# A sixth buffer for the experts' down weights, the overflow table summed on TensorE, and another order of capacities in a one-core decoder step

## The reference

```python
def moe(h, w_router, b_router, we_g, we_u, we_d, ws_g, ws_u, ws_d):
    s = jax.nn.sigmoid(jnp.dot(h, w_router).astype(jnp.float32))
    ...                                   # group-limited top-8 of 64 experts for each token
    def step(acc, blk):
        e, tok, wt = blk                  # expert, its rows of h, their weights
        xb = h[tok]
        hb = jax.nn.silu(xb @ we_g[e]) * (xb @ we_u[e])
        return acc.at[tok].add(wt[:, None] * (hb @ we_d[e]).astype(jnp.float32)), None
    ...
    shared = (jax.nn.silu(h @ ws_g) * (h @ ws_u)) @ ws_d
    return (routed + shared.astype(jnp.float32)).astype(h.dtype)
```

## Time and profile before

| | |
|---|---|
| profiled execution | 1106.16 us |
| its span (first to last instruction of the profile) | 1104.3 us |
| median of three runs | 1107.29 us |
| PE busy | 1063.3 us (96%) |
| VectorE busy | 730.3 us (66%) |
| first gate/up matmul of block 0 | 487.64 us |
| last down matmul of block 47 ends | 1041.1 us |
| moved by DMA in the whole execution | 337.11 MB |

### The profile page before, as it was taken

How to read it: one execution, slowest core, us unless ns; L and a number is a source line. 1 busy time by engine, 2 the same in 40 slices (tenths; PEclk the granted TensorE clock), 3 DMA queues, 4 the chain that set the end, 5 groups by cost and what they waited for, 6 DMA issues and landing times.

```text
span 1104.3 us, 16558 instructions
## 1 busy us (share of the span) xinstructions
PE 1063.3 (96%) x5950; PEld 533.5 (48%) x5950; DVE 730.3 (66%) x1935; ACT 215.4 (20%) x473; POOL 135.6 (12%) x163
## 2 busy tenths in 40 slices
PE   6999999999999999999999999999899999999896
PEld 3456678777877644664433333333233333333232
DVE  3218441546545645766988888888687988888167
ACT  4131332222232313301111111111010111111111
POOL 0110000000020010111111111111111212121100
PEclk9999999999999999999999999999999999999999
DMA  9858720120352267769999999999999999999698
GB/s 368 340 200 302 241 81 27 50 86 1 115 191 87 77 243 249 284 281 382 413 411 425 421 426 425 424 422 425 425 425 425 421 424 424 413 417 407 261 417 353
DMA packets 51653, 337.11 MB, mean 305 GB/s; under 512 B 9636, under 2 KB 14088, under 8 KB 30830
## 3 DMA queue, kind: packets, MB, share of 16 engines
q1 hardware_dynamic: 33710, 287.32, 64.1%
q0 software_dynamic: 17856, 48.68, 11.5%
HBM read 311.30 MB, written 37.24 MB: 316 GB/s over the span
## 4 chain that ended last, share of the span: by engine, by line
PE 82%; DMA 11%; DVE 4%; issue 1%; ACT 1%; SPq 0%; DVEq 0%; ACTq 0%
PE bank L1599 24%; PE bank L1622 13%; PE bank L1294 10%; DMA mem<-in_w_exp_down 6%; PE bank L1313 5%; PE bank L1412 3%; DMA hT<-in_w_exp_down 3%; PE bank L1413 3%; PE bank L1207 3%; PE bank L1530 3%; PE bank L1291 3%; DMA mem<-expert_out_rows 2%; PE bank L1708 2%; PE bank L1182 1%; PE bank L1610 1%
## 5 line engine op out<-in xcount | busy, mean ns | idle before, releaser
L1599 PE MATMUL bank<-mem 128*32 128x512 f32 (+2 forms) x1568 | 334.0, 595 | 1.8 <-DVE mem L2291 1.0
L2291 DVE STREAM_TRANSPOSE mem<-mem 32x256 f32<-32x256 f32 x448 | 195.1, 436 | 5.8
L1622 PE MATMUL bank<-mem 128*32 128x512 f32 (+2 forms) x712 | 178.7, 602 | 9.2 <-DMA mem<-in_w_exp_down 5.7
L1599 PEld LDWEIGHTS bank<-mem 128*32 128x32 f32 (+2 forms) x1568 | 106.9, 128 | 165.0 <-issue 164.9
L1294 PE MATMUL bank<-hT,mem 128*128 128x288 f32 x512 | 133.3, 410 | 1.0 <-ACT mem L973 1.0
L2291 DVE STREAM_TRANSPOSE mem<-x_sb 32x256 f32<-32x256 f32 x240 | 104.5, 435 | 3.1
L1294 PEld LDWEIGHTS bank<-hT,mem 128*128 128x128 f32 x512 | 93.8, 190 | 25.8 <-issue 2.4
L1622 PEld LDWEIGHTS bank<-mem 128*32 128x32 f32 (+2 forms) x712 | 56.6, 132 | 80.3 <-issue 71.2
L1599 PE MATMUL bank<-x_sb,mem 128*32 128x512 f32 (+2 forms) x256 | 87.1, 596 | 0.0
L2307 DVE COPY hT<-bank 128x512 f32<-128x512 f32 x48 | 33.2, 691 | 66.6 <-PE bank L1622 66.5
L827 POOL DMA_INDIRECT mem<-ffn_in_rows,idxg x32 | 33.0, 1030 | 268.2 <-DVE idxs L2275 192.8
(11 more groups left out here) (398 smaller groups left out, 1215.5 us busy)
## 6 DMA issues: line engine op xcount, KB each, us to landing
mem<-k_w_exp SPq DMA_DIRECT2D x54, 2048.0 KB
mem<-in_w_exp_down SPq DMA_DIRECT2D x52, 1024.0 KB
x_sb<-k_w_exp SPq DMA_DIRECT2D x10, 2048.0 KB
mem<-k_w_ada SPq DMA_DIRECT2D x8, 2048.0 KB, 9.3
mem<-k_w_in SPq DMA_DIRECT2D x7, 2048.0 KB, 9.5
hT<-in_w_exp_down SPq DMA_DIRECT2D x12, 1024.0 KB
mem<-expert_out_rows SPq DMA_DIRECT2D x6, 2048.0 KB, 18.1
mem<-k_w_head SPq DMA_DIRECT2D x4, 2048.0 KB, 17.2
```

Of the source, the lines that this page charges most:

```text
L1599: i = mm(bank[sl, :], xT[:, j % 2, c * BLK + sl.start:c * BLK + sl.stop], gu_view(r)[:, c, :], start=c == 0, stop=c == KC - 1)
L1622: i = mm(ps[4 + hf][sl, :], hhT[:, k * BLK + sl.start:k * BLK + sl.stop], dn_view(r)[:, k, hf * 512:(hf + 1) * 512], start=k == 0, stop=k ...
L2291: i = dve.transpose(cols[dl, :, sl], rows[sl, :, dl])
```

## The change

Four things are changed.

1. `CAPS` has other numbers in another order, and `PRE` is `[0, 1, 5, 21]` in place of `[0, 1, 4, 5]`. The sum is 192 units as before, and the multiset of the 60 capacities outside `PRE` is the same (7, 6, four 5s, nine 4s and so on). The blocks that the two tables give are: before 18 whole, 12 in two pieces of 64, 18 in four of 32; after 8 whole, 11 in two, 29 in four. The fourth preloaded expert is first used in block 15.
2. The down weights get a sixth place: 2048 columns of `aux`, which held the router's scratch. The scratch that is left moves behind column 3072.
3. The large operations of `table` go. VectorE makes two columns on 64 partitions, TensorE sums over the partitions with two small matmuls behind the down matmuls of block 4, and VectorE finishes the table in block 6.
4. SyncE reads a rank's expert number (a TENSOR_LOAD) ahead of each load in place of once a rank, and issues the down loads of free places ahead of the wait for the shared expert.

```diff
-PRE = [0, 1, 4, 5]
-CAPS = [4, 4, 2, 2, 4, 4, 2, 2, 2, 2, 4, 5, 3, 4, 3, 5, 2, 2, 3, 1,
+PRE = [0, 1, 5, 21]
+CAPS = [4, 4, 1, 2, 4, 4, 1, 3, 2, 2, 4, 4, 3, 3, 3, 3, 4, 2, 2, 3,
...
-WSLOTS = 5
+WSLOTS = 6
...
-        DN_AT = [gate_at, 2 * KC * FE, WSZ + 2 * KC * FE, w2_at, None]
+        DN_AT = [gate_at, 2 * KC * FE, WSZ + 2 * KC * FE, w2_at]
...
-        assert at <= NO * NE
-        ocmp, at = carve(aux, 0, [NO, NE])
-        cape, at = carve(aux, at, [NE])
+        AUX_FREE = 3 * D
+        assert at <= AUX_FREE
+        dnA, _ = carve(aux, 0, [FJ, D])
+        cape, at = carve(aux, AUX_FREE, [NE])
...
-            ids = {r: sp.value_load(ptab[0:1, r:r + 1], min_val=0, max_val=NE - 1) for r in (early, late)}
-            load_gate_up(early, ids[early])
+            free = [r for r in range(NE) if r not in PRE and DN_BEFORE[r] is None]
+            assert [DN_PLACE[r] for r in free] == list(range(len(PRE), WSLOTS))
+            load_gate_up(early, ranked(early))
+            for r in free[:-1]:
+                load_dn(r, ranked(r))
             sp.wait_ge(S["gu_mm"], NSH)
-            load_gate_up(late, ids[late])
-            load_dn(early, ids.pop(early))
+            load_gate_up(late, ranked(late))
+            load_dn(free[-1], ranked(free[-1]))
...
+            def table_sums():
+
+                pe.wait_ge(S["tbl_ready"], 2)
+                mm(ps[0][:, 0:NO], ones[0:NE, :], tge[0:NE, :], start=True, stop=True)
+                mm(ps[0][:, NO:2 * NO], twt[0:NE, :], tge[0:NE, :], start=True, stop=True).then_inc(S["tbl_mm"], 1)
...
                     down(b - 1, pieces(b - 1))
+                if b == TURNED:
+                    table_sums()
...
                 if part == 1:
-                    step(dve.tensor_reduce(ovs[:, 0, :], ocmp, AX.X, ALU.add))
-                    step(tt_(ocmp, ocmp, wrow.unsqueeze(1).to_broadcast([P, NO, NE]), ALU.mult))
-                    return
-                if part == 2:
-                    step(dve.tensor_reduce(ovs[:, 1, :], ocmp, AX.X, ALU.add))
+                    dve.wait_ge(S["tbl_mm"], 2)
+                    step(cp(ovs[:, 0:2, :], ps[0][:, 0:2 * NO].rearrange("p (a s) -> p a s", a=2)))
...
-                s_ = iota[:, 0:NO]
-                step(tt_(ocmp, s_.unsqueeze(2).to_broadcast([P, NO, NE]), cnt.unsqueeze(1).to_broadcast([P, NO, NE]), ALU.is_ge))
+                for i, v in enumerate((cnt, wrow)):
+                    step(tt_(tsq[0:NE], v[0:NE], ident[0:NE, 0:NE], ALU.mult))
+                    step(dve.tensor_reduce(tcol[0:NE, i:i + 1], tsq[0:NE], AX.X, ALU.add))
+                step(ts(tge[0:NE], iota[0:NE, 0:NO], tcol[0:NE, 0:1], None, ALU.is_ge))
+                ts(twt[0:NE], ones[0:NE, :], tcol[0:NE, 1:2], None, ALU.mult).then_inc(S["tbl_ready"], 1)
...
-                if 1 <= b <= 3:
-                    table(b - 1)
+                if b in (1, TURNED + 1):
+                    table(b // TURNED)
```

More of the change, by code:

```diff
@@ L39 @@
 QS = 32
-PRE = [0, 1, 4, 5]
-CAPS = [4, 4, 2, 2, 4, 4, 2, 2, 2, 2, 4, 5, 3, 4, 3, 5, 2, 2, 3, 1,
-        6, 3, 3, 2, 5, 2, 3, 4, 1, 3, 2, 2, 4, 4, 2, 3, 3, 3, 2, 3, 5, 3, 4, 3, 3, 2, 3, 2,
-        3, 7, 3, 2, 4, 4, 3, 2, 3, 2, 2, 4, 2, 2, 1, 3]
+PRE = [0, 1, 5, 21]
+CAPS = [4, 4, 1, 2, 4, 4, 1, 3, 2, 2, 4, 4, 3, 3, 3, 3, 4, 2, 2, 3,
+        2, 4, 3, 2, 5, 3, 2, 5, 2, 4, 3, 4, 2, 2, 3, 6, 3, 4, 3, 2, 7, 4, 4, 3, 3, 2, 3, 2,
+        3, 2, 1, 3, 5, 2, 3, 2, 2, 3, 5, 3, 2, 2, 2, 2]
 NBK = sum(CAPS) * QS // BLK
@@ L377, in build @@
         lgS, at = carve(aux, at, [2 * P + NS])
-        assert at <= NO * NE
-        ocmp, at = carve(aux, 0, [NO, NE])
-        cape, at = carve(aux, at, [NE])
+        AUX_FREE = 3 * D
+        assert at <= AUX_FREE
+        dnA, _ = carve(aux, 0, [FJ, D])
+        cape, at = carve(aux, AUX_FREE, [NE])
         wrow, at = carve(aux, at, [NE])
+        tsq, at = carve(aux, at, [NE])
+        tge, at = carve(aux, at, [NO])
+        twt, at = carve(aux, at, [P])
+        tcol, at = carve(aux, at, [2])
         assert at <= len(GRN) * T
@@ L398, in build @@
             P_ready idx_mm idx_ready gat0 gat1 gat2 xgT_t xgT_a xT_ready eup egs ehh ehT_t ehT edn eout_a eout_d sct0 sct1
-            ld_gu0 ld_gu1 ld_gu2 ld_gu3 ld_gu4 ld_d0 ld_d1 ld_d2 ld_d3 srt_ready srt_mm over yp_mm yh0 yh1 yh2 yh3 yh4 yh5 yh6 yh7 yd_sum yl_sum yf_rt x2_done out_st dch ach pch""".split()
+            ld_gu0 ld_gu1 ld_gu2 ld_gu3 ld_gu4 ld_d0 ld_d1 ld_d2 ld_d3 tbl_ready tbl_mm over yp_mm yh0 yh1 yh2 yh3 yh4 yh5 yh6 yh7 yd_sum yl_sum yf_rt x2_done out_st dch ach pch""".split()
         S = {n: sem(n) for n in names}
@@ L503, in dn_view @@
         def dn_view(r):
-            at_ = DN_AT[place_of(r, DN_PLACE)]
-            return dnX if at_ is None else mem[:, at_:at_ + FJ * D].rearrange("p (j d) -> p j d", j=FJ)
+            p = place_of(r, DN_PLACE)
+            if p < len(DN_AT):
+                return mem[:, DN_AT[p]:DN_AT[p] + FJ * D].rearrange("p (j d) -> p j d", j=FJ)
+            return dnX if p == WSLOTS - 1 else dnA
         GU_LOADED = [("ld_a1", 32), ("ld_gu0", 0), ("ld_gu1", 0), ("ld_gu2", 0), ("ld_gu3", 0), ("ld_gu4", 0)]
-        DN_LOADED = [("ld_a2", 32), ("ld_d0", 0), ("ld_d1", 0), ("ld_d2", 0), ("ld_d3", 0)]
+        DN_LOADED = [("ld_a2", 32), ("ld_d0", 0), ("ld_d1", 0), ("ld_d2", 0), ("ld_d3", 0), ("ld_a4", 16 * NSL)]
         def gu_sem(r):
@@ L664, in _, with ranked @@
             sp.wait_ge(S["tab_ready"], 1)
+            def ranked(r):
+                return sp.value_load(ptab[0:1, r:r + 1], min_val=0, max_val=NE - 1)
             early, late = [r for r in range(NE) if r not in PRE and GU_BEFORE[r] is None]
-            assert GU_PLACE[early] == XSLOT and GU_PLACE[late] == LATESLOT and DN_PLACE[early] == XSLOT
-            ids = {r: sp.value_load(ptab[0:1, r:r + 1], min_val=0, max_val=NE - 1) for r in (early, late)}
-            load_gate_up(early, ids[early])
+            assert GU_PLACE[early] == XSLOT and GU_PLACE[late] == LATESLOT
+            free = [r for r in range(NE) if r not in PRE and DN_BEFORE[r] is None]
[3 more added lines that the diff above has]
+                load_dn(r, ranked(r))
             sp.wait_ge(S["gu_mm"], NSH)
-            load_gate_up(late, ids[late])
-            load_dn(early, ids.pop(early))
+            load_gate_up(late, ranked(late))
+            load_dn(free[-1], ranked(free[-1]))
             for when, is_dn, r in sorted([(LASTB[q] + 0.5, 0, r) for r, q in enumerate(GU_BEFORE) if q is not None] +
                                          [(LASTB[q] + 2.0, 1, r) for r, q in enumerate(DN_BEFORE) if q is not None]):
+                e = ranked(r)
                 if not is_dn:
-                    ids[r] = sp.value_load(ptab[0:1, r:r + 1], min_val=0, max_val=NE - 1)
                     sp.wait_ge(S["eup"], LASTB[GU_BEFORE[r]] + 1)
-                    load_gate_up(r, ids[r])
+                    load_gate_up(r, e)
                 else:
                     sp.wait_ge(S["edn"], LASTB[DN_BEFORE[r]] + 1)
-                    load_dn(r, ids.pop(r))
+                    load_dn(r, e)
             sp.wait_ge(S["eup"], last_use(EXTSLOT) + 1)
@@ L1649, in _ @@
             pe.wait_ge(S["sh_ready"], 2)
-            pe.wait_ge(S["srt_ready"], 1)
+            pe.wait_ge(S["tbl_ready"], 1)
             mm(ps[7][:, 0:2 * NE], ones[0:NE, :], sperm[0:NE].rearrange("p a e -> p (a e)"),
-               start=True, stop=True).then_inc(S["srt_mm"], 1)
+               start=True, stop=True).then_inc(S["tbl_mm"], 1)
             shared_up(KC // 2)
```

4 lines of the change are left out of this document (2 added, 2 removed).

## The result

The changed kernel takes 1117.68 us (median of 4, 1115.73 to 1118.87) against 1106.82 us for the kernel before (4 runs, 1104.44 to 1107.92). The ratio is 1.0099, 95% interval 1.0084 to 1.0114: 11 us slower, where 1105.8 us and a range up to 1110.3 had been forecast. The profiled execution took 1118.87 us, its span 1117.1.

A forecast was written before the change was run, and what follows sets the result against it. TensorE and DMA both full, DMA slightly tighter. TensorE's terms sum to 11.1 us late against 12.7; DMA's account gains 1.3 us. Taking 1.5 off 1107.29 gave 1105.8 us, 8-in-10 range 1101.3 to 1110.3.

The forecast's parts named there:

- The table: Moving the table off VectorE removes block 5's 1.0 us wait; two small matmuls cost TensorE 0.3 us.
- Split blocks: Ten more blocks are split, at 0.2 us each: 2.0 us more, range 0 to 4.
- the arrival of the weights: Each load's landing time, counted from bytes, gathers and scatters ahead of it; early by 4 us in mid-stage, fitting at block 47.
- block 2: At its start, a new 1.9 us wait for rank 4's gate/up weights, times 1.5: 3 us.
- blocks 13 and 16: At block 16, rank 23's down weights come 0.9 to 5 us late, taken as 2.5; block 13 had no term.
- block 39: A wait for weights of 0 to 3 us, taken as 1.
- waits of before that go: Waits at blocks 5, 24, 25, 29 and 36 go, which had made PE 12.7 us late at the end.
- no idle DMA behind 530 us: DMA share stays 1.0 from 530 to 1030 us; idle slices in mid-stage would make the forecast wrong.
- (b): Rival: block 2 starves the DMA queue, DMA idles 5 us against 1.5, giving 1110.8 us; chance 0.22.
- (a): Rival: weight supply has slack at the stage's end, so fewer waits count, 4.6 us less, 1102.7 us; chance 0.24.
- (c): Rival: the sixth down buffer does nothing since DMA is full; new waits equal the old, 1107.3 us; chance 0.10.
- The factor for the clock: Each PE wait costs 1.5 times its length, from 10.1 us lost for waits of 6.6 us.

The follow-up runs named there:

- e1: The changed kernel with the old `CAPS` and `PRE` put back, so only the sixth down buffer and the table on TensorE remain; 1103.59 us.
- e8: The changed kernel with each down load into a place used before bringing only half of its bytes; 1099.97 us.
- e9: The changed kernel with valid slots of each quarter of 32 spread evenly over eight groups of four partitions, a list of ranks filled from the other end; 1108.68 us.
- e11: The changed kernel with ranks 0, 1, 4, 5 preloaded, filled as in e9 with its own list of ranks; 1108.15 us.
- e14: e9 with another list of ranks filled from the other end, so that empty slots gather in alternate quarters and the halves fill alike; 1109.21 us.
- e17: The changed kernel in its own order, each rank filled in one of four ways, counted excess 8 slots or less at every block; 1108.66 us.
- e16: e1 with each rank filled in one of four ways, so that by count no engine is more than 4 slots over the mean; 1101.68 us.
- e13: e9 with another list of ranks filled from the other end, so that empty slots gather in one half of 64 slots; 1124.67 us.
- e7: The changed kernel with ranks 0, 1, 4, 5 preloaded in place of 0, 1, 5, 21; 1116.91 us.

## Why the prediction was wrong, step by step

**What held.** Two resources full at once, and the loss comes out at blocks 2, 16, 39, 41 and the last one, where the count had placed the tight spots (block 13 it had not). The waits of blocks 5, 24, 25, 29 and 36 all went. The table, by the result copies of e1 against those of before: block 5's wait was worth 1.1 us (1.0 was said), the two matmuls lengthened block 5 by 0.6 (0.3). Split blocks: with the table's matmuls 1.8 us by e8; 2.0 and 0.3 were said. Ten more blocks are split, as was said, and eleven more are in four pieces. VectorE's extra ranks cost nothing: its idle time ahead of the result copies even grew, 66.6 us in the earlier trace rows to 72.1:

```profile
L2328 DVE COPY hT<-bank 128x512 f32<-128x512 f32 x48 | 33.2, 691 | 72.1 <-PE bank L1635 72.1
```

**The step that failed: the arrival of the weights.** The prediction counted bytes as one stream into one queue: "488.3 + MB / 0.4204 + 1.03 for each gather and scatter + 1.5". It had found this count 4 us early against rank 33's load and took that as a constant error of mid-stage, to be added at block 16 (0.9 to 5, I took 2.5) and dropped at the end, where it seemed to fit. The completions show what was counted, the mean engine, and what PE waits for, the last one:

| load | by the count | mean of its 16 completions | last |
|---|---|---|---|
| before, rank 33's down | 787.9 | 786.6 | 792.0 |
| before, the last gate/up | 1024.5 | 1015.1 | 1022.3 |
| after, rank 23's down | 689.4 | 689.5 | 696.9 |
| after, the last gate/up | 1023.6 | 1024.1 | 1037.3 |

The 4 us were most of the way from the mean engine to the last, 5.4 us. That way isn't constant; it depends on the table of capacities, which sets where the empty slots lie: the fullest engine is 11 slots over the mean before and 16 after at block 15, 21 and 52 at block 41. The fit at the end was luck: the count was 9 us late there against the mean, and the last gate/up load landed 2.6 us before PE wanted it, at 1024.9. In the changed kernel, with the same bytes ahead of it, it landed 15 us later. The prediction had named the drift ("if the slowest DMA engine trails"), and rightly left it out at block 2, where the 16 completions lie within 2.4 us; what it did not ask is whether the change alters it. The terms that rest on it are the ones that are off, measured by the result copies against the same blocks of e8 (block 2 against the kernel before):

| term | predicted | measured |
|---|---|---|
| block 2 | 3 | 4.6 |
| blocks 13 and 16 | 2.5 | 1.9 + 7.2 |
| block 39 | 1 | 6.8 |
| block 41 | 2 | 0.9 |
| behind block 41 | 0 | 1.9 |
| table, splits, place | 2.6 | 1.8 + 0.3 |
| waits of before that go | -12.7 | -12.8 |

The right column sums to 12.6 us at the end of the stage, and the last copy came 12.5 us later. Of the 10.9 us between the two kernels, levelling takes away 9.0 (e9). What is left isn't the forecast gain of 1.5 us: the levelled kernels with the new order stay 0.17 to 0.23% above the kernel before (e9, e11, e14, e17), with waits at block 16 and, in most, at 2 and 41. In e9's profiled execution the stage, from block 0's copy to block 47's, takes 532.6 us, against 532.7 before and 544.9 in the changed kernel; that the forecast's 1.5 us don't come is the order's own demand for weights, as e17 against e16 has it. Behind the last copy e9 needs 2.7 us more than the kernel before (65.8 against 63.1), and nothing on record explains these.

**The second failure: no idle DMA behind 530 us.** The forecast named idle slices in mid-stage as what would refute it, and they came, at 860 to 900 us. Engines that are ahead have done all that was issued, while the buffers stay taken until the slowest is through. That is a part of it: levelled, the share is 0.98 and 392 GB/s move (e9); apart on purpose, it is lower (e13). The other part is the new order's: e17, the most level of all, has 0.94 and 367 GB/s there, while e1, with the old order, has 1.01 and 424.

```profile
860.00:900.00 40.00, 40.00 (x402) 13.96 (x398) 35.95 (x96) 4.87 (x11) 6.72 (x7) 1.00 0.90 352
```

So running apart costs twice: the last part of each load is late, and the faster engines lose time that they don't get back. How the 9.0 us divide between the two was not measured.

**The rivals.** (b), that block 2 starves the queue, was right in its mechanism: block 2 started at 511.57, before the 512.5 from which I had let it decide, and the queue still stood empty for 2.5 us. But its price is nearly nothing, as e7 and e11 show; what that pause takes is taken again at block 16. (a) had its premise half right, since before there were 2.6 us of slack at block 47; after there were none, and PE waited 1.8 us. (c) was wrong about the buffer, which is worth about 2.5 us in the old order and 16 in the new.

**The factor for the clock.** 1.5 was about right: block 39's 3.8 us of wait cost 6.8, block 16's 4.4 cost 7.2, block 2's 2.9 cost 4.6, so 1.6 to 1.8.

## What to carry to other kernels

A transfer that is split over parallel engines ends with the slowest of them; where other traffic skips work unevenly (masked rows in a gather or scatter), count the load of each engine and not only the bytes. The completions of one load, one for each engine, show the drift directly, and a look at them would have shown it in the kernel before. When a count of bytes agrees at the end and is some us off in the middle, that residue is a mechanism and has to be explained before it is carried into another configuration. And a wait taken away ahead of a stretch that another resource bounds, as block 2's here, comes back at the next tight spot.
